# Moving two modulation chunks of a two-block transformer kernel from the value stage to the query and key stage

## The reference, cut to what matters

```python
proj = rms_norm(x, norm1_g) @ w_in           # q, k, v, z, xbc, dt, two gates
q = rms_norm(q.reshape(B, S, 16, 64), q_norm_g); k = rms_norm(k..., k_norm_g)
x = x + mixed @ w_out
x = x + peer_ffn(rms_norm(x, norm2_g), ...)  # 128 blocks "pu" in, 128 blocks "pv" out
...
mod = silu(c) @ ada_w[layer] + ada_b[layer]              # [1024] @ [1024, 6144], two layers
mod_c = silu(c_ctx) @ ada_w[0] + ada_b[0]
h_ctx = modulate(rms_norm(ctx, norm_mix_w), cshift, cscale)
h = modulate(rms_norm(x, norm_mix_w), shift, scale)
```

## Time and profile before

| what | us |
| --- | --- |
| median of three executions | 2185.55 |
| the profiled execution, its own time | 2185.88 |
| its span, first to last instruction | 2184.1 |
| busy: PE, DVE, ACT, GpSimd | 2117.2, 1538.8, 1121.8, 274.9 |
| chain that ended last: PE, DVE, ACT, DMA | 81%, 8%, 5%, 2% |
| mean granted clock of PE | 0.979 |

### The profile page before, as it was taken

One profiled execution on the slowest core, in us unless ns is written; L12 is line 12 of the kernel. 1 busy time (PEld: TensorE's weight loads), 2 busy tenths in 40 slices (PEclk: granted clock), 3 DMA queues, 4 the chain that ended last, 5 costly groups with the idle time before them and its releaser, 6 DMA issues.

```text
span 2184.1 us, 40308 instructions
## 1 busy us (share of the span) xinstructions
PE 2117.2 (97%) x16826; PEld 2042.7 (94%) x16826; DVE 1538.8 (70%) x2684; ACT 1121.8 (51%) x1740; POOL 274.9 (13%) x256
## 2 busy tenths in 40 slices
PE   8999999999999999999999999999998999999998
PEld 7898899999998999999999999998878999999998
DVE  6787689775995777886777586573456886766764
ACT  5566677545444666654443454562245553445553
POOL 0000000002899445410000000000000000000000
PEclk9999999999999999999999999999899999999999
DMA  5433433667554444457767676322015677554553
GB/s 196 162 132 127 134 123 116 212 197 243 188 184 165 141 142 144 139 181 235 241 230 260 222 248 235 112 91 89 29 35 173 243 246 247 196 193 150 185 173 116
DMA packets 104005, 375.43 MB, mean 172 GB/s; under 512 B 11536, under 2 KB 12176, under 8 KB 103184
## 3 DMA queue, kind: packets, MB, share of 16 engines
q1 hardware_dynamic: 103824, 372.86, 50.8%
HBM read 370.71 MB, written 2.10 MB: 171 GB/s over the span
## 4 chain that ended last, share of the span: by engine, by line
PE 81%; DVE 8%; ACT 5%; DMA 2%; POOL 2%; issue 1%; SPq 0%; DVEq 0%; ACTq 0%
PE ps L365 23%; PE ps L366 22%; PE ps L367 22%; DVE wl L1458 3%; PE ps L724 3%; POOL wl L2153 2%; ACT wh L1027 1%; PE ps L449 1%; DVE arena L1582 1%; PE ps L521 1%; PE ps L433 1%; PE ps L434 1%; PE ps L435 1%; PE ps L818 1%; PE ps L837 1%
## 5 line engine op out<-in xcount | busy, mean ns | idle before, releaser
L365 PE MATMUL ps<-xah,wh 128*128 128x256 f32 x2944 | 844.5, 287 | 16.3 <-DVE xal L1483 5.4
L366 PE MATMUL ps<-xal,wh 128*128 128x256 f32 x2944 | 832.5, 283 | 0.0
L367 PE MATMUL ps<-xah,wl 128*128 128x256 f32 x2944 | 831.8, 283 | 0.0
L1458 DVE TENSOR_TENSOR wl<-raw,wh 128x1024 fp32r<-128x1024 f32 (+2 forms) x548 | 644.7, 1197 | 208.8 <-ACT wh L1027 207.4
L1027 ACT ACTIVATE wh<-raw 128x1024 fp32r<-128x1024 f32 (+1 forms) x608 | 620.6, 1036 | 322.7 <-PE ps L367 198.4
L365 PEld LDWEIGHTS ps<-xah,wh 128*128 128x128 f32 x2944 | 560.7, 190 | 29.0 <-issue 18.4
L366 PEld LDWEIGHTS ps<-xal,wh 128*128 128x128 f32 x2944 | 561.0, 191 | 0.5 <-issue 0.2
L367 PEld LDWEIGHTS ps<-xah,wl 128*128 128x128 f32 x2944 | 560.5, 190 | 0.0
L365 PE MATMUL ps<-hh,wh 128*128 128x256 f32 x1024 | 292.1, 285 | 10.3 <-DVE wl L1458 8.6
L366 PE MATMUL ps<-arenar,wh 128*128 128x256 f32 x1024 | 289.8, 283 | 0.0
L367 PE MATMUL ps<-hh,wl 128*128 128x256 f32 x1024 | 289.7, 283 | 0.0
(11 more groups left out here) (330 smaller groups left out, 2927.7 us busy)
## 6 DMA issues: line engine op xcount, KB each, us to landing
raw<-in_pu SPq DMA_DIRECT2D x128, 512.0 KB, 3.3
raw<-in_pv SPq DMA_DIRECT2D x128, 512.0 KB, 3.6
raw<-in_ada SPq DMA_DIRECT2D x96, 512.0 KB, 4.3
raw<-in_ff_up SPq DMA_DIRECT2D x88, 512.0 KB, 3.6
raw<-in_w_xbc SPq DMA_DIRECT2D x32, 512.0 KB, 3.3
raw<-in_ff_down SPq DMA_DIRECT2D x32, 512.0 KB, 4.0
raw<-in_w_z SPq DMA_DIRECT2D x16, 512.0 KB, 3.3
raw<-in_w_so SPq DMA_DIRECT2D x16, 512.0 KB, 3.9
```

The costliest lines, as they stand in the source:

```text
L365: mm(o, w0, x0, start=start, stop=False, skip_group_check=skip)
L366: mm(o, w0, x1, start=False, stop=False, skip_group_check=skip)
L367: return mm(o, w1, x0, start=False, stop=stop, skip_group_check=skip)
L1458: tt_(W.lo(i), W.raw(i), W.hi(i).bitcast(f32), ALU.subtract).then_inc(S["lowV"], 1)
```

## The change

Chunks (0, 4) and (0, 5) get a stage of their own, "qk". In PE's program a step stands in the middle of each of the tiles 2 to 7 and after each unit of the values; in DVE's, at the end of turns 2 to 7 (behind `head(i - 1)`) and after the `lows` of each values unit. The ten chunks left in "pv" take 14 blocks where the context needs them too, 8 otherwise, and 19 for the last two (before: 13, 8 and 10). CTX goes from 80 to 86.

```diff
-        MO = {"so": CHUNKS[:4], "pv": [(0, c) for c in (0, 4, 1, 5, 2, 6, 3, 7, 8, 9, 10, 11)], "ff": CHUNKS[4:12]}
+        MO = {"qk": [(0, 4), (0, 5)], "so": CHUNKS[:4], "pv": [(0, c) for c in (0, 6, 1, 7, 2, 8, 3, 9, 10, 11)],
+              "ff": CHUNKS[4:12]}
...
-        STEPS, CTX, at = set(), 80, 0
+        STEPS, CTX, at = set(), 86, 0
         for n, chunk in enumerate(MO["pv"]):
-            blocks = 13 if both(*chunk) == 2 else 8 if n < 8 else 10
+            blocks = 14 if both(*chunk) == 2 else 8 if n < 8 else 19
             STEPS.update(at + blocks * q // 5 for q in range(5))
...
+            mq = modulation("qk", range(6))
             for i in range(8):
...
-                    tile(("qk", i), ("w_q", "w_k")[i // 4], 2 * (i % 4), 8, XA, n1, range(6))
+                    tile(("qk", i), ("w_q", "w_k")[i // 4], 2 * (i % 4), 8, XA, n1, range(6), mq)
...
             for c in range(2):
-                run(rows(("v", c), "w_v", c, xt, range(6)))
+                for _ in rows(("v", c), "w_v", c, xt, range(6)):
+                    next(mq, None)
...
+            mq = modulation("qk")
             for i in range(8):
                 lows(B.units[("qk", i)] + AHEAD)
                 if i:
                     head(i - 1)
+                if i > 1:
+                    next(mq)
             head(7)
             for c in range(2):
-                lows(B.units[(("v", c), 1)] + AHEAD)
+                for u in range(4):
+                    lows(W.at[("v", c), "w", u] + 1 + AHEAD)
+                    next(mq, None)
+            run(mq)
```

More of the change, by code:

```diff
@@ L295, in build @@
         CHUNKS = [(1, c) for c in range(12)] + [(0, c) for c in range(12)]
-        MO = {"so": CHUNKS[:4], "pv": [(0, c) for c in (0, 4, 1, 5, 2, 6, 3, 7, 8, 9, 10, 11)], "ff": CHUNKS[4:12]}
-        MODN = {lc: n for n, lc in enumerate(MO["so"] + MO["pv"] + MO["ff"])}
-        ACCS = {"so": acc1, "pv": accp, "ff": accf}
+        MO = {"qk": [(0, 4), (0, 5)], "so": CHUNKS[:4], "pv": [(0, c) for c in (0, 6, 1, 7, 2, 8, 3, 9, 10, 11)],
+              "ff": CHUNKS[4:12]}
+        MODN = {lc: n for n, lc in enumerate(MO["qk"] + MO["so"] + MO["pv"] + MO["ff"])}
+        ACCS = {"qk": acc1, "so": acc1, "pv": accp, "ff": accf}
         BESIDE = [([("z", 1)], []), ([("z", 2)], [("ga", 0)]), ([("z", 3)], []), ([("z", 4)], [("ga", 1)]),
```

## The result

| | before | after |
| --- | --- | --- |
| median, us | 2185.45 (2185.26 to 2186.07, 4 runs) | 2213.43 (2212.88 to 2214.01, 4 runs) |
| ratio, 95% interval | | 1.013 (1.0117 to 1.0143) |
| profiled span | 2184.1 | 2211.1 |
| values start | 73.2 | 106.2 |
| attention starts | 96.7 | 131.7 |

The change costs 28.0 us; 2218 was forecast and the range held it. The shift from before to after is +35.0 us at attention, +34.3 where the expert values start, +25.3 at their end and +27.0 at the end of the program. So queries to values lose 35.0, the expert values give back 9.0, and the rest is 0.7 off and 1.7 on.

What follows compares the result with a forecast made beforehand. PE, busy for 97% of the span, was taken to bound the kernel. Queries to values +31.8, the clock there +6 and the expert values -5.5 made +32.3 us on 2185.9: 2218 us, range 2199 to 2234.

Steps and rivals of the forecast that it cites:

- queries to values: Stretch up to attention's start: claimed 31.8 us longer, through slower tiles, the sum of (0, 4) and bank 1.
- the expert values: Stage that gives two chunks away: claimed -5.5 us, a 3.7 us stand cut to 1.2 and its lower clock gone.
- The sum: Whole kernel: 31.8 + 6 - 5.5 = +32.3 us on the profiled execution's 2185.9, said as 2218.
- The front stage: Queries to values, which takes in chunks (0, 4) and (0, 5): +31.8 us, plus 6 for the clock there.
- The round: Ring slot's way in the tiles: step, load, rounding, copy, square, root and head claimed 11.8 us against a 6.62 us tile.
- The milestones: Start times along queries to values: first one-column matmuls near 81, values near 104 and attention near 128.5 us.
- the term of the clock: Lower clock behind two stands, the sum's and the values': 2 x 3 = +6 us, between 0 and 12.
- bank: Start of the values: bank 1 holds the sums of (0, 4) until `columns`, so values start at 104.0, before 73.17.
- DVE's time alone: Rival, front stage: slot back early, bank no hindrance, only DVE's 11.4 us more work counts; 2189 us, chance 0.08.
- Faster: Rival: the front stage hides both chunks and the expert values give back all 11.6 us; 2174 us, chance 0.02.
- The values' stage is not helped: Rival, expert values: the context's transfers delay another unit as long; 2224 us, inside the range, within the forecast's 0.80.
- The clock stays low: Rival, front stage: PE stays at the slow level, 28 us in place of 6; 2240 us, chance 0.07.

## Why the prediction was right

The sum was +32.3 us; the traces show +27.0 and the medians +28.0. The front stage cost 2.8 us less than forecast, the expert values gave back 3.5 more, and 1.0 us was lost elsewhere.

**The round: right.** 11.8 us forecast, 12.0 measured. From the trace of after: the step ends at 57.01, ACT starts at 60.72 (3.7, where I had 3.5), low half, copy and root make 63.53 (2.8 after that), the head and the step 5.5. Every term but the load is the row's.

**The milestones: right, each a little late.**

| start of | forecast, without the clock | measured |
| --- | --- | --- |
| first sum | 80.9 | 81.3 |
| head 5 | 86.4 | 88.6 |
| head 6 | 93.0 | 95.2 |
| values | 104.0 | 106.2 |
| attention | 128.5 | 131.7 |

Head 5 is 2.2 us late, and 1.8 of that arise between the sum and head 5 (7.3 us where I had 5.5), for the most part by the clock. These stretches of after show it at its half level (1.2 GHz) with PE in series:

```profile
83.30:86.70 3.40, 3.40 (x18) 3.40 (x17) 0.00 (x0) 0.00 (x0) 0.00 (x0) 0.50 0.96 345
100.40:110.60 10.20, 4.38 (x10) 3.51 (x11) 9.33 (x10) 1.06 (x1) 0.00 (x0) 0.50 0.32 104
```

Half of 3.4 us is 1.7. The second stretch starts inside the stand and lasts 4.4 us beyond its end, which costs 2.2. The clock therefore took 3.9 us where I had 6: **the term of the clock was too large by half**, because I laid a whole stretch of 6 us behind each stand. The first lasted only 3.4 us, and 5.8 us of the second passed during the stand, when they cost nothing. The values' units took what was left: (131.68 - 106.22) less 2.2 is 23.3 us, 1.2 less than the 24.5 forecast. With its clock the front stage was forecast at 37.8 and took 35.0.

**What of it was bank and what was round: not seen.** The sum was right, but the prediction reads as if the values would start at once with the bank free. The kernel with another bank got back 3.3 of 10.4 us in its trace, and only with the step ahead of the head as well did 22 us return.

**The expert values: right in kind, 9.0 us instead of 5.5.** The stand of 3.7 became 1.3 (0.28 and 1.02); 1.2 was forecast. That it fits so well is partly luck: in the six other kernels with the same expert values the stands at this place were 0.8 to 2.7 us in sum. None of them had half clock there, as forecast. Before had 6.8 us of it, from 1179.3, and 1.7 of these passed during the stand, so 2.6 us were lost where I had 3.0. Not in the forecast: the other stands are 0.9 us less in sum, and at the context's mean, which I costed at nothing, the half clock held 3.4 us instead of 6.8 (1.7 us). These make 7.6 of the 9.0; the rest I can't name. Behind the stage after has 6.8 us at half where before had 3.4, which loses 1.7 again. The stretches at the context's mean and behind the stage differ from one kernel's trace to the next by as much, so I take these two for chance. What the order of the transfers gives by itself was measured, 0.9977, and what CTX gives, 0.9989.

**The rivals.** DVE's time alone, 2189: no, since the kernel with 8 columns is as slow as after. A kernel near that case exists, the version with the step ahead of the head and another bank (1.0037 of 2185.45 is 2193.5). Faster: no. The values' stage is not helped: no, it gave back 9.0 us. The clock stays low: from 46 to 106 us PE was busy 37.2 us of 60, and the mean clock was 0.78, not 0.5:

```profile
46.00:106.00 60.00, 37.18 (x210) 33.04 (x210) 42.20 (x33) 19.49 (x27) 0.00 (x0) 0.78 0.40 140
```

The rule of the Trainium skill that I had weighed ("TensorE: Matmul & The Clock Gate", Part 1), by which the slow level is the default and activity releases it, agrees with the direction: every slow stretch of this stage starts in or behind a stand. But the clock came back each time; no slow stretch of this stage was longer than 10.2 us.

## What to carry to other kernels

When background work shares a ring with the main loads, what counts is where in the other engine's turn it gives its slot back: behind the head of 4 us, 1.45 us of work cost 5.4 us a tile (12.0 against 6.6), ahead of it 1.1 (7.8). Follow the slot round the ring by the queue's order before counting work, and give a side computation a bank that the next stage doesn't start with. A wait that is removed can uncover another (behind the bank's 10.4 us stood one of 5.9), so undo causes together before you call one small.

A burst of transfers in a shared queue delays the load that stands right behind it (8.28 us to land, where the median was 4.3); moving the burst behind that load was worth 0.23% for one changed number.

## What the runs showed of the hardware that I had not expected

The clock falls during a stand and not only after it. In after, PE stood from 95.8 to 106.2, and the granted clock was at its half level from 100.4 on (stretches of after; the clock is the number behind POOL's):

```profile
95.80:100.30 4.50, 0.00 (x0) 0.00 (x0) 4.43 (x4) 1.63 (x2) 0.00 (x0) 1.00 0.00 0
100.40:106.20 5.80, 0.00 (x0) 0.01 (x1) 5.73 (x7) 0.53 (x1) 0.00 (x0) 0.50 0.55 181
106.20:110.60 4.40, 4.38 (x10) 3.50 (x11) 3.60 (x4) 0.53 (x1) 0.00 (x0) 0.50 0.01 4
```

So a slow stretch costs less than its length suggests: 5.8 of these 10.2 us passed while PE stood, and only the 4.4 us of matmuls right behind ran slowly.

It can also fall without a stand. In before, PE worked on the one-column matmuls of the context's mean without a stand from 1241.4 to 1245.7 us, and the clock was at its half level from 1244.1 on, for 6.8 us.

DVE's multiply-add on 8 columns took 0.22 us against 0.75 on 512: a 64th of the columns, nearly a third of the time. So a thin step still cost 0.40 of its 1.45 us.

The reciprocal on DVE took 3.35 us for 128x512, the multiply-add of the same size 0.75 us. In the round of 12.0 us it is the longest operation, only the load's 3.57 us from issue to landing is longer, and the slot had to wait behind it.
